# Where the operands of TensorE lie in SBUF, modulo 512 bytes: activations and three block sums change places

## The chip, the cores and the metric

The kernel runs on one core of one Trainium2 chip. Time is device microseconds of one execution, from runs on the chip; three runs of the kernel before gave 1962.86, 1964.51 and 1965.04 us. Lower is better. SBUF is the on-chip memory that the engines read: each of its 128 partitions is a row of bytes, and "address" below is the byte within a partition at which a buffer begins.

## The reference

One decoder layer in float32 on 512 tokens of 2048 features. What is computed:

```python
proj = x @ w_in                               # 2048 -> 4180, split among four head groups
mix  = concat(pooling, conv module, DSA attention, NSA attention)
x = LN(alpha * x + mix @ w_out)               # 2048 x 2048
gate, up = split(x @ w_gate_up)               # 2048 -> 2 x 5632
x = LN(alpha * x + (silu(gate) * up) @ w_down)  # 5632 -> 2048
```

The last two lines, the feed-forward part, are where the change has its largest place.

## The kernel before

**Three products for one.** Each large matrix is used in two parts, a high part (the float32 rounded to the matmul type fp32r) and a low part (the rest). A product is made of three passes that accumulate in PSUM: high by high, high by low, low by high. So every tile of weights is a triple of matmuls, on three lines of code that follow one another. A matmul has a stationary operand (128x128, loaded into the array by its own weight load, LDWEIGHTS, PEld in the profile) and a moving operand (128x256 or 128x512) that streams through.

**Stages in order.** (1) The input projection, `feature_slab` and `part_slab`, lines 799 to 801 through the helper `passes`: stationary is a "whole slab" of weights (`w_hi`, `w_lo`), moving the activations `act`, 512 columns. (2) The attention and pooling parts, on other buffers. (3) The output projection, `out_tile`, lines 1034 to 1036: stationary `act`, moving the slab, 512 columns; in its last quarter two of four slabs lie in `spare_1` and `spare_2`, which are parts of `x_room`. (4) The first two gate and up chunks, again lines 799 to 801: the first pair in halves of 256 columns, the second in 512; the slab of one of them lies in `xs_4`. (5) From 710 us to 1906 us the feed-forward part: 42 chunk units and 20 down units, in the order that `ff_units` writes out (three chunks, two downs, one chunk, and again).

**A chunk unit** makes gate and up of 128 features by seven block products instead of eight (Strassen's scheme). Each is 8 weight tiles by 3 passes = 24 matmuls of 256 columns, on lines 1152, 1154 and 1156 (`product`). The stationary operand is always a piece of the weight ring (`ring_hi`, `ring_lo`, in `w_room`). The moving operand is: product 0, `act`; products 1 and 2, the block sums s1 and s2 in `x_room`; product 3, the block sum s4 in `xs_4` (the trace writes xs); product 4, the block sum s3, which is kept in `act`; products 5 and 6, `act`. So 4 of 7 have `act` as moving operand and 3 of 7 the sums in `x_room` and `xs_4`.

**A down unit** has seven block products of 12 matmuls of 512 columns, lines 1201, 1203 and 1205: stationary the hidden blocks (`h01`, `h23`, `hs4`, `hs21`), moving the weight ring. The tail (lines 1241 to 1243) is the last part of the down product, with moving operands from the ring and from `late`, which begins at the start of `x_room`.

**Who feeds the ring.** SP issues the DMAs, ACT writes the high part (line 1490), VectorE the low part (line 2041) and the weights' block sums (lines 2049 to 2056). Semaphores count all of it, and each engine's order is written out by hand.

**Where the buffers lie.** Buffers are laid out one after the other, so a constant early in the layout moves what follows. `w_room` begins at byte 2240, which is 192 modulo 512. The ring is cut from its start in pieces of 4096 bytes, the low half 512 bytes further, so every piece of the ring is at 192 modulo 512. `SHIFT` (floats, 4 bytes each) says how far past the ring's start the whole slabs begin, and, since `act` and `raw` follow `w_room` and `between` fills up to a fixed sum, also where these two lie. `X_SHIFT` says how far past the start of `x_room` (192 modulo 512) the block sums s1 and s2 begin; `xs_4` and the rows of gain and bias follow `x_room`. The matmul operands step from tile to tile by multiples of 512 bytes, so an operand keeps its place modulo 512.

| buffer | used as | before, mod 512 | past the ring | after, mod 512 | past the ring |
|---|---|---|---|---|---|
| weight ring | stationary (chunk), moving (down, tail) | 192 | 0 | 192 | 0 |
| `w_hi`, `w_lo` whole slabs | stationary (1, 4), moving (3) | 224 | 32 | 256 | 64 |
| `act` (also holds s3) | moving (1, 4, chunk), stationary (3) | 224 | 32 | 256 | 64 |
| s1, s2 and the spare slabs in `x_room` | moving (chunk, 3) | 256 | 64 | 224 | 32 |
| s4 / a slab in `xs_4` | moving (chunk), stationary (4) | 256 | 64 | 224 | 32 |
| hidden blocks, `late` in `x_room`, `raw_c`, `proj` | as named above | 192 | 0 | 192 | 0 |

Of the kernel before, what the change touches and what calls it, by code (L numbers as in the profile page):

```python
# [98 lines left out]


GRAN = SLAB // 2
SHIFT = 8
X_SHIFT = 144
HALF_TOKS = SEQ // 2
S_ORDER = ("s1", "s2", "s4", "s3")
TAIL_SLOTS = ((0, 32), (2, 32), (4, 63), (5, 63), (1, 32), (3, 32), (0, 33), (2, 33))
# [36 lines left out]
def build(nc, x, x_t, w_in, w_out, pool_w, pool_scale, conv_w, conv_b, conv_ln_g, conv_ln_b, conv_pw_w,  # L143
          conv_pw_b, cmp_pos_k, cmp_pos_v, cmp_k_w1, cmp_k_w2, cmp_v_w1, cmp_v_w2, ln1_g, ln1_b,
          ln2_g, ln2_b, w_gate_up, w_down, out):
    with ExitStack() as ctx:
        def sb(name, shape, dt=F32, where=ctx):
            return where.enter_context(nc.sbuf_tensor(name, shape, dt))

        def sem(name):  # L150
# [5 lines left out]
        std = sb("std", [P, TT])  # L156
        w_room = sb("w_room", [P, 4 * SLAB + P + SHIFT], F32R)
        w_hi, w_lo = (w_room[:, SHIFT + at:SHIFT + at + 2 * SLAB].rearrange("p (s n) -> p s n", s=2)
                      for at in (0, 2 * SLAB + P))
# [3 lines left out]

        between = sb("between", [P, P - SHIFT])

# [50 lines left out]
        with a2_scope:  # L216
            below_s1 = sb("below_s1", [P, X_SHIFT], F32, a2_scope)
            s1 = sb("s1", [P, KT // 2, HALF_TOKS], F32, a2_scope)
            below_a2 = sb("below_a2", [P, SLAB], F32, a2_scope)
            a21 = sb("a21", [P, KT // 2, HALF_TOKS], F32, a2_scope)  # L220
            a22 = sb("a22", [P, KT // 2, HALF_TOKS], F32, a2_scope)
        x_room = sb("x_room", [P, 4 * SLAB + X_SHIFT], F32R, feed)
        xs_1, xs_2 = (x_room[:, X_SHIFT + at:X_SHIFT + at + 2 * SLAB].rearrange("p (a k n) -> p a k n", a=2, n=HALF_TOKS)
                      for at in (0, 2 * SLAB))
# [5 lines left out]
        with s4_scope:  # L230
# [22 lines left out]
        spare_1, spare_2 = ((x_room[:, at:at + SLAB], x_room[:, at + SLAB:at + 2 * SLAB])  # L253
                            for at in (X_SHIFT, X_SHIFT + 2 * SLAB))
        spare_4 = tuple(xs_4[:, a, :, :].rearrange("p k n -> p (k n)") for a in range(2))
# [2005 lines left out]
```

How the kernel before makes its waits and increments, by code:

```python
        def copied(eng, n):  # L451
            eng.wait_ge(bank_free[n % 2], n // 2 + 1)
# [1 line left out]
        def tile_ready(eng, group, slab, i):  # L455
            if i < TT - 1:
                eng.wait_ge(tile_done, group * (TT - 1) + (i + 1))
            else:
                eng.wait_ge(slab_done, slab + 1)
# [4 lines left out]
        @block.sync  # L465
# [19 lines left out]
            rows = ((conv_w[0], 0, CONV_WIDTH), (conv_b, V_CB, 1), (conv_ln_g, V_LG, 1),  # L485
                    (conv_ln_b, V_LB, 1), (conv_pw_b, V_PB, 1), (pool_scale, V_PS, 1))
            for src, at, n in rows:
                nc.sync.dma_start(sel[at:at + n, 0:SEQ], src).then_inc(small_loaded, 16)
            nc.sync.dma_start(sel[0:CMP_BLOCK, SEQ:SEQ + P], cmp_pos_k[0]).then_inc(small_loaded, 16)
            nc.sync.dma_start(sel[CMP_BLOCK:2 * CMP_BLOCK, SEQ:SEQ + P], cmp_pos_v[0]).then_inc(small_loaded, 16)
            nc.sync.dma_start(w2[:, 0, :], cmp_k_w2[0]).then_inc(small_loaded, 16)
            nc.sync.dma_start(w2[:, 1, :], cmp_v_w2[0]).then_inc(small_loaded, 16)
            for n in (2, 3):
                sp.wait_ge(part_lo, n + 3)
                load(n % 2, win[:, :, C_IQ + n * P:C_IQ + (n + 1) * P], KT)
            sp.wait_ge(split_done, N_IKWG - 1)
            ikwg = raw[:, 0, 0:KT * (W_IKW + W_NG)].rearrange("p (k n) -> p k n", k=KT)
# [2 lines left out]
            with sp.Fori(0, 4) as c:
                sp.wait_ge(split_done, 2 * c + (N_CONV - 1))
                load(1, win[:, :, bass.ds(c * P + C_G, P)], KT)
```

## Time and profile before

| | us |
|---|---|
| median of three runs (lowest, highest) | 1964.51 (1962.86, 1965.04) |
| the profiled execution's own time | 1964.08 |
| its span | 1962.2 |
| PE busy | 1952.2 (99%) |
| PE weight loads | 1731.7 (88%) |
| VectorE, ACT, POOL busy | 1412.2, 848.4, 504.1 |

The 1.9 us between the time and the span lie around the program's own instructions. TensorE's granted clock is 1.0 in every slice, which is its upper level of 2.4 GHz. The "mean ns" of a matmul group is the length of one matmul with its way through the array, and matmuls overlap; what a matmul costs a stream is the distance from its start to the start of the next. That distance is read in the timeline, as the difference of two start times divided by the number of matmuls between.

### The profile page before, as it was taken

Reading aid. Unit: us, or ns where it says so; the run is one execution under the profiler, and the core shown is the slowest. Engines: PE = TensorE matmul, PEld = TensorE weight load, DVE = VectorE, ACT = ScalarE, POOL = GpSimd, SP = SyncE. Lnnn points to the kernel's source line nnn. Section 1 sums busy time; section 2 is a strip of 40 time slices with the busy share of each in tenths; the row PEclk is TensorE's granted clock in tenths of the full one; section 3 lists DMA queues with packets and bytes.
Section 4 is the critical chain, followed back from the end, with each engine's and each line's share of the span. In section 5 each row is a group of like instructions: output and inputs, shape, how many; then the busy total and the mean of one; then the engine's idle time right before and its main releaser. Section 6 shows DMA issues by size and latency. Waiting matters only on the chain.

```text
span 1962.2 us, 30226 instructions
## 1 busy us (share of the span) xinstructions
PE 1952.2 (99%) x12301; PEld 1731.7 (88%) x12301; DVE 1412.2 (72%) x1911; ACT 848.4 (43%) x1280; POOL 504.1 (26%) x343
## 2 busy tenths in 40 slices
PE   9999999999999999999999999999999999999998
PEld 7777888866888999998989999899998989999896
DVE  3079997274112988887878888888788888878777
ACT  3011001265000545556565555655555555555553
POOL 2555656244567310202011020201102020110200
PEclk9999999999999999999999999999999999999999
DMA  7433343500524524938557394754839376493972
GB/s 214 105 89 80 92 103 90 177 21 25 214 86 131 170 65 129 184 118 166 136 130 172 114 187 126 156 149 116 186 98 203 111 158 152 111 200 90 204 244 87
DMA packets 316429, 264.28 MB, mean 135 GB/s; under 512 B 12262, under 2 KB 258854, under 8 KB 313482
## 3 DMA queue, kind: packets, MB, share of 16 engines
q1 hardware_dynamic: 292026, 211.97, 37.7%
q0 software_dynamic: 23616, 46.15, 14.1%
q10 hardware_dynamic: 656, 4.33, 0.6%
q8 instruction: 93, 1.52, 0.3%
q14 instruction: 38, 0.31, 0.1%
HBM read 211.95 MB, written 50.33 MB: 134 GB/s over the span
## 4 chain that ended last, share of the span: by engine, by line
PE 96%; DMA 1%; DVE 1%; ACT 1%; issue 0%; SPq 0%; DVEq 0%
PE psum L1152 14%; PE psum L1156 14%; PE psum L1154 14%; PE psum L799 7%; PE psum L801 7%; PE psum L800 7%; PE psum L1201 6%; PE psum L1203 6%; PE psum L1205 6%; PE psum L1034 3%; PE psum L1035 3%; PE psum L1036 3%; PE psum L1013 1%; PE psum L950 1%; PE psum L941 1%; PE psum L1001 1%
## 5 line engine op out<-in xcount | busy, mean ns | idle before, releaser
L2041 DVE TENSOR_TENSOR w_room<-raw,w_room 128x1024 fp32r<-128x1024 f32 x310 | 379.5, 1224 | 158.9 <-ACT w_room L1490 158.8
L1490 ACT CAST w_room<-raw 128x1024 fp32r<-128x1024 f32 x312 | 329.1, 1055 | 211.3 <-DVE raw L2052 70.3
L769 POOL DMA_DIRECT2D out<-stage x160 | 139.5, 1472 | 1017.5 <-DVE stage L2152 996.8
L1152 PE MATMUL psum<-act,w_room 128*128 128x256 f32 x1344 | 375.7, 280 | 0.0
L1154 PE MATMUL psum<-act,w_room 128*128 128x256 f32 x1344 | 375.4, 279 | 0.0
L1156 PE MATMUL psum<-act,w_room 128*128 128x256 f32 x1344 | 375.3, 279 | 0.0
L1152 PEld LDWEIGHTS psum<-act,w_room 128*128 128x128 f32 x1344 | 252.6, 188 | 0.4
L1154 PEld LDWEIGHTS psum<-act,w_room 128*128 128x128 f32 x1344 | 252.6, 188 | 0.4
L1156 PEld LDWEIGHTS psum<-act,w_room 128*128 128x128 f32 x1344 | 252.8, 188 | 0.0
L799 PE MATMUL psum<-act,w_room 128*128 128x512 f32 (+2 forms) x608 | 231.8, 381 | 1.7 <-DVE act L1716 1.2
L800 PE MATMUL psum<-act,w_room 128*128 128x512 f32 (+2 forms) x608 | 230.0, 378 | 0.0
L801 PE MATMUL psum<-act,w_room 128*128 128x512 f32 (+2 forms) x608 | 229.9, 378 | 0.0
L677 POOL TENSOR_TENSOR w_room<-raw,w_room 128x2048 fp32r<-128x2048 f32 (+1 forms) x45 | 207.4, 4609 | 3.8
L1152 PE MATMUL psum<-x_room,w_room 128*128 128x256 f32 x672 | 185.6, 276 | 0.0
L1156 PE MATMUL psum<-x_room,w_room 128*128 128x256 f32 x672 | 185.5, 276 | 0.0
L1154 PE MATMUL psum<-x_room,w_room 128*128 128x256 f32 x672 | 185.5, 276 | 0.0
L2041 DVE TENSOR_TENSOR w_room<-raw_c,w_room 128x1024 fp32r<-128x1024 f32 x124 | 151.6, 1223 | 46.9 <-ACT w_room L1490 45.1
L674 POOL TENSOR_SCALAR w_room<-raw 128x2048 fp32r<-128x2048 f32 (+1 forms) x45 | 88.9, 1975 | 259.5 <-PE psum L801 136.9
L799 PEld LDWEIGHTS psum<-act,w_room 128*128 128x128 f32 (+1 forms) x608 | 113.8, 187 | 26.9 <-issue 4.4
L800 PEld LDWEIGHTS psum<-act,w_room 128*128 128x128 f32 (+1 forms) x608 | 113.8, 187 | 22.1 <-issue 0.5
L801 PEld LDWEIGHTS psum<-act,w_room 128*128 128x128 f32 (+1 forms) x608 | 113.8, 187 | 22.1
L1490 ACT CAST w_room<-raw_c 128x1024 fp32r<-128x1024 f32 x126 | 132.9, 1055 | 0.0
(303 smaller groups left out, 4121.5 us busy)
## 6 DMA issues: line engine op xcount, KB each, us to landing
raw_c<-in_w_gate_up SPq DMA_DIRECT2D x84, 512.0 KB, 6.6
raw<-in_w_gate_up SPq DMA_DIRECT2D x84, 512.0 KB, 5.8
out<-stage POOLq DMA_DIRECT2D x160, 256.0 KB, 8.2
raw<-in_w_in SPq DMA_DIRECT2D x30, 1024.0 KB, 5.8
raw<-in_w_down SPq DMA_DIRECT2D x46, 512.0 KB, 4.8
raw_c<-in_w_down SPq DMA_DIRECT2D x42, 512.0 KB, 4.4
raw<-in_w_out SPq DMA_DIRECT2D x16, 1024.0 KB, 5.1
acc<-in_x SPq DMA_DIRECT2D x1, 4096.0 KB, 12.5
```

The costliest lines, as they stand in the source:

```text
L677: nc.gpsimd.tensor_tensor(lo, raw[:, slot, 0:words], hi.bitcast(F32), ALU.subtract)\
L769: nc.gpsimd.dma_start(out_dram[:, tile, n * SEQ:(n + 1) * SEQ], part, accum_op=ALU.add)\
L799: nc.tensor.matmul(out_ap, stat_hi, mov_hi, start=first, stop=False)
L800: nc.tensor.matmul(out_ap, stat_hi, mov_lo, start=False, stop=False)
L801: return nc.tensor.matmul(out_ap, stat_lo, mov_hi, start=False, stop=last)
L1152: nc.tensor.matmul(out_ap, stat_hi[:, cols], mov_hi[:, k, :], start=opens and k == 0, stop=False, skip_group_check=not opens)
L1154: nc.tensor.matmul(out_ap, stat_hi[:, cols], mov_lo[:, k, :], start=False, stop=False, skip_group_check=not opens)
L1156: mm = nc.tensor.matmul(out_ap, stat_lo[:, cols], mov_hi[:, k, :], start=False, stop=k == kh - 1, skip_group_check=not opens)
L1201: nc.tensor.matmul(out_ap[:, i, :], room[:, 0, j, toks], w_h[:, cols], start=opens and j == 0, stop=False, skip_group_check=not opens)
L1203: nc.tensor.matmul(out_ap[:, i, :], room[:, 1, j, toks], w_h[:, cols], start=False, stop=False, skip_group_check=not opens)
L1490: nc.scalar.copy(ring_hi(at), src).then_inc(hi_ready, 1)
L2041: nc.vector.tensor_tensor(lo, src, hi.bitcast(F32), ALU.subtract).then_inc(lo_ready, 1)
```

## The change

Two constants change. `SHIFT` goes from 8 to 16 floats (32 to 64 bytes), `X_SHIFT` from 144 to 8 floats (576 bytes, which is 64 modulo 512, to 32 bytes). `act` and `raw` begin 32 bytes later, the whole slabs too; s1, s2, the spare slabs, `xs_4` and the gain and bias rows begin 544 bytes earlier. The sequence of instructions is the same on each of the five engines, row for row; only the addresses differ.

```diff
 GRAN = SLAB // 2
-SHIFT = 8
-X_SHIFT = 144
+SHIFT = 16
+X_SHIFT = 8
 HALF_TOKS = SEQ // 2
```

Where they are used:

```python
w_room = sb("w_room", [P, 4 * SLAB + P + SHIFT], F32R)
w_hi, w_lo = (w_room[:, SHIFT + at:SHIFT + at + 2 * SLAB]... for at in (0, 2 * SLAB + P))
between = sb("between", [P, P - SHIFT])
below_s1 = sb("below_s1", [P, X_SHIFT], F32, a2_scope)
x_room = sb("x_room", [P, 4 * SLAB + X_SHIFT], F32R, feed)
```

## Rows read from the trace of the kernel before

**Rows 1.** The page, part 1: busy us (share of the span) xinstructions.
```profile
PE 1952.2 (99%) x12301; PEld 1731.7 (88%) x12301; DVE 1412.2 (72%) x1911; ACT 848.4 (43%) x1280; POOL 504.1 (26%) x343
```

**Rows 2.** Windows: length, busy PE PEld DVE ACT POOL (xinstructions), PEclk, DMA share, GB/s.
```profile
710.50:1905.90 1195.40, 1195.40 (x8738) 1129.67 (x8737) 984.52 (x1113) 672.77 (x914) 142.22 (x166) 1.00 0.62 149
```

**Rows 3.** Timeline of PE, third chunk unit: start, length, engine, line, op, names.
```profile
749.91 0.28 PE L1152 MATMUL psum<-act,w_room 128*128 128x256 f32 x1
...
752.71 0.28 PE L1152 MATMUL psum<-x_room,w_room 128*128 128x256 f32 x1
...
760.88 0.28 PE L1152 MATMUL psum<-act,w_room 128*128 128x256 f32 x1
...
769.29 0.40 PE L1201 MATMUL psum<-w_room,h 128*128 128x512 f32 x1
```

**Rows 4.** Timeline of PE, first and second chunk unit.
```profile
710.54 0.28 PE L1152 MATMUL psum<-act,w_room 128*128 128x256 f32 x1
...
713.34 0.28 PE L1152 MATMUL psum<-x_room,w_room 128*128 128x256 f32 x1
...
721.82 0.28 PE L1152 MATMUL psum<-act,w_room 128*128 128x256 f32 x1
...
730.46 0.28 PE L1152 MATMUL psum<-act,w_room 128*128 128x256 f32 x1
...
733.34 0.28 PE L1152 MATMUL psum<-x_room,w_room 128*128 128x256 f32 x1
```

**Rows 5.** Timeline of PE, end of the second down unit.
```profile
788.35 0.39 PE L1201 MATMUL psum<-w_room,h 128*128 128x512 f32 x1
...
807.39 0.28 PE L1152 MATMUL psum<-act,w_room 128*128 128x256 f32 x1
```

**Rows 6.** Timeline of PE, stage 4: halves, the slab in xs_4, the slab in w_room.
```profile
673.73 0.28 PE L800 MATMUL psum<-act,w_room 128*128 128x256 f32 x1
...
688.00 0.40 PE L799 MATMUL psum<-act,xs 128*128 128x512 f32 x1
...
699.19 0.39 PE L799 MATMUL psum<-act,w_room 128*128 128x512 f32 x1
...
710.08 0.62 PE L1142 MATMUL psum<-act 128*128 128x512 f32 x2
```

**Rows 7.** Timeline of PE, output projection: from w_room, then from x_room.
```profile
500.11 0.39 PE L1034 MATMUL psum<-w_room,act 128*128 128x512 f32 x1
...
624.55 0.40 PE L1034 MATMUL psum<-x_room,act 128*128 128x512 f32 x1
...
630.15 0.40 PE L1034 MATMUL psum<-w_room,act 128*128 128x512 f32 x1
```

**Rows 8.** Timeline of PE, tail: moving operand from late, in x_room.
```profile
1944.98 0.39 PE L1241 MATMUL psum<-x_room,h 128*128 128x512 f32 x1
...
1950.19 0.39 PE L1243 MATMUL psum<-x_room,h 128*128 128x512 f32 x1
```

**Rows 9.** Lines of VectorE and ACT by form, 900 to 1900 us: busy, mean ns, idle before.
```profile
L2041 DVE TENSOR_TENSOR w_room<-raw,w_room 128x1024 fp32r<-128x1024 f32 x259 | 317.1, 1224 | 133.1 <-ACT w_room L1490 133.0
L2041 DVE TENSOR_TENSOR w_room<-raw_c,w_room 128x1024 fp32r<-128x1024 f32 x104 | 127.2, 1223 | 41.3 <-ACT w_room L1490 39.9
...
L1490 ACT CAST w_room<-raw 128x1024 fp32r<-128x1024 f32 x260 | 274.2, 1055 | 176.9 <-DVE raw L2052 60.6 <-DVE raw L2049 54.7 <-PE psum L1156 48.8
L1490 ACT CAST w_room<-raw_c 128x1024 fp32r<-128x1024 f32 x104 | 109.7, 1055 | 0.0
```

**Rows 10.** Lines of PE by form, whole span: busy, mean ns, idle before.
```profile
L1152 PE MATMUL psum<-act,w_room 128*128 128x256 f32 x1344 | 375.7, 280 | 0.0
...
L1152 PE MATMUL psum<-x_room,w_room 128*128 128x256 f32 x672 | 185.6, 276 | 0.0
...
L799 PE MATMUL psum<-act,w_room 128*128 128x256 f32 x64 | 18.3, 286 | 0.0
...
L1034 PE MATMUL psum<-x_room,act 128*128 128x512 f32 x32 | 12.7, 398 | 0.0
```

## Prediction

> **What bounds the kernel now.** I read the page's first part, then one sum over the feed-forward part, then the timeline. TensorE is busy for 1952.2 of 1962.2 us [rows 1]; from 710.5 to 1905.9 us it never stops (1195.40 of 1195.40 us, granted clock 1.00, the upper level of 2.4 GHz), while VectorE works 984.5 and ACT 672.8 us of it [rows 2]. So in 61% of the span no wait can be removed, and none is near: the time is the number of matmuls times the distance from one start to the next. The change alters no instruction, only addresses, so it can act through that distance alone.
>
> The distance is read from start times. In the third chunk unit [rows 3] the 24 matmuls of product 0 (moving operand in `act`) take 749.91 to 752.71 = 2.80 us, 116.7 ns each; the 72 of products 1 to 3 (moving in `x_room`, `xs_4`) take 8.17 us, 113.5 ns; the 72 of products 4 to 6 (moving in `act` again) 8.41 us, 116.8 ns. Same shape, same stationary ring, same clock; the moving operand's place differs: 32 bytes past the ring in `act`, 64 in the sums. That is the only term of size.
>
> **Is it the place, or the buffer?** Four other readings say the place. (a) Same two buffers, 256 columns, but a whole slab in place of a ring piece, hence offset 0 between stationary and moving: 673.73 to 688.00, 119 matmuls, 119.9 ns [rows 6]. So 0, 32 and 64 bytes give 119.9, 116.7 and 113.5 ns. (b) At 512 columns offset 0 costs nothing over twice 113.3: `act` with `w_room` 226.7 ns (500.11 to 624.55, 549 matmuls) [rows 7], and 226.9 with the roles exchanged (48 matmuls) [rows 6]. (c) `x_room` as moving operand 32 bytes past `act` takes 233.3 ns (24 matmuls) [rows 7], yet the same `x_room` at offset 0 to the hidden blocks takes 226.5 (23 distances) [rows 8]. (d) `act` moving 32 bytes before `xs_4` takes 233.1 (48) [rows 6]. A buffer that is slow in one pairing is at the floor in another. Down units have both operands 192 modulo 512 and run at 226.7 (84 matmuls, 19.04 us) [rows 5]; nothing in them moves.
>
> Here a rule of the Trainium skill speaks against the change. Its page "TensorE: Matmul & The Clock Gate" (step-by-step, on LDWEIGHTS) says that TensorE has two independent read ports and that loading the next weights takes no read bandwidth from the running matmul. By that rule the places of the two operands could not matter and the change would be worth 0. The trace disagrees in so far as the same matmul takes 113.5, 116.8 or 119.9 ns; whether the reads meet in a bank no row shows.
>
> **Part by part.**
>
> 1. *Chunk units, `act` from 32 to 64 bytes past the ring.* Products 4 to 6 go from 8.41 to what products 1 to 3 take now, 8.17; product 0 from 2.80 to a third of 8.17 = 2.72.
> 2. *Chunk units, the sums from 64 to 32.* Products 1 to 3 go from 8.17 to 8.41. Terms 1 and 2 together: a unit goes from 19.38 (749.91 to 769.29) to 2.72 + 8.41 + 8.17 = 19.30. The exchange of three against three cancels; what stays is one product, 4 against 3, at 0.077 us. All on the path, nothing beside it: 42 x 0.077 = -3.2 us. The bound of that term: no trace shows `act` at 64 or the sums at 32, so `act` gives between 0 and 42 x 96 x 3.3 ns = -13.3 us, the sums cost between 0 and 42 x 72 x 3.3 ns = +10.0 us. I take both in full, for (a) to (d).
> 3. *The first two units.* They aren't like the others [rows 4]: products 1 to 3 of unit one run at 117.8 ns (721.82 - 713.34 over 72) at the same addresses that give 113.5 later, products 4 to 6 and the next unit's product 0 at 120.0, and only at 733.34 does the fast pace begin. Unit one takes 19.92 us, unit two 19.45; against 19.38 that is 0.61 us too much. So a pairing has a slow and a fast rhythm (117.8 or 113.5 at 64 bytes; 120.0 or 116.8 at 32), which the stream falls into by how it arrives, and keeps. After the change the stream arrives otherwise: between 0 and -0.6 us; I take -0.3.
> 4. *Whole slabs with `act`* (input projection, most of the output projection, the first chunks). Both move by 32 bytes, the offset stays 0: 0 us. (b) and the down units show offset 0 at 226.7 both at 224 and at 192 modulo 512, so the absolute place isn't what counts. If 256 in place of 224 did lift the half-width pairs of [rows 6] to 113.5, it would be 119 x 6.4 ns = -0.8 us.
> 5. *Spare slabs in `x_room`, slab in `xs_4`.* The first go from +32 to -32 relative to `act`, the second from -32 to +32. +32 measures 233.3 and -32 233.1, so 96 and 48 matmuls trade nothing: 0 us, 0.1 at most.
> 6. *VectorE, ACT, DMA.* `raw` moves from 224 to 256, `act` too. VectorE's subtraction takes 1224 ns from `raw` (at 224) and 1223 from `raw_c` (at 192), ACT's cast 1055 from both [rows 9]: their place costs nothing. They get 0.08 us less per unit of 19.38 and VectorE is busy 82% of the stretch [rows 2], so no wait opens; were VectorE the limit, it would show as TensorE's first idle time there.
>
> Sum: -3.2 - 0.3 = -3.5 us. The profiled execution took 1964.08 us (span 1962.2 and 1.9 around it); it would take 1960.6. The median of the three runs lies 0.4 higher at 1964.51: forecast 1961.0 us, a span of 1958.7. What a measurement of this kernel tells from no change is about 0.2%, here 3.9 us, so the forecast sits just short of that edge.
>
> **Rivals.**
>
> *R1, the slow rhythm after each down group (no change).* Product 0 after a down unit is reached from a stream at 226.7 ns. At 32 bytes it settles at once at 116.8; at 64 nobody has seen this entry. If it falls into 117.8 as in unit one, product 0 costs 24 x 4.4 ns = 0.11 more, products 1 to 3 follow at 120.0 as products 4 to 6 did there, 72 x 3.2 = 0.23, and product 4 escapes as at 733.34. Eleven entries (the start and ten down groups) x 0.34 = +3.7, against -3.2: 1965.0. For it: unit one. Against: the rows hold one entry into 64 bytes that ends slow (713.34) and two that end fast, 733.34 from the slow rhythm [rows 4] and 752.71 from the fast one [rows 3].
>
> *R2, the penalty belongs to `act`, and the sums catch one too (slower).* `act` steps by 2048 bytes between weight tiles, the sums by 1024, and `act` lies next to the ring. If that is what makes 116.8, `act` stays there at 64 bytes, while the sums at 32 rise to it: 42 x 72 x 3.3 ns = +10.0, 1974.5 us. It decides if product 0 stays at 116 ns or more. Against it: (a), where the same buffers give 119.9 at another offset.
>
> *R3, the slow rhythm everywhere (slower).* Units of 96 x 117.8 + 72 x 120.0 ns = 19.95 against 19.38: 42 x 0.57 = +24, 1988 us. Against it: each entry from `act` to the sums after unit one is fast, and after the change product 4 is entered in just that way, 32 to 64 bytes, after a multiple of 24 matmuls.
>
> *R4, the sums don't mind 32 bytes.* Their tiles lie closer; then only term 1 counts: -13.3, 1951 us. For it: only `act` has been seen at 32 with the ring. Against: (c), (d).
>
> *R5, the places don't matter* (the rule of the page named above would give this time too): 1964.5 us. Against it: (a) to (d).
>
> **How the numbers follow.** The exchange as worked out 58%, R1 18%, R4 8%, R2 8%, R3 3%, R5 5%. The first gives -3.2 to -4.6 us, with terms 3 and 4 at their ends, and the three runs spread over 2.2 us, so the edge at -3.9 cuts it near the middle: 27 of the 58 fall over 0.2% faster, 31 within. Faster: 27 + 8 = 35%. Same: 31 + 18 + 5 = 54%. Slower: 8 + 3 = 11%. The range 1957.5 to 1966.5 holds the first, R1 and R5, 81%; R2, R3 and R4 lie outside.
>
> **What would show it.** In the timeline of the third unit after: product 0 in 2.72 us, products 1 to 3 in 8.41, products 4 to 6 in 8.17, the unit in 19.30. In the groups by line, the mean for `act` at L1152 falls from 280 to 276 ns and that for x_room rises from 276 to 280, while the spare slabs at L1034 stay at 398 and the halves at L799 at 286 [rows 10]. Units one and two tell of term 3, product 0 after 807 us of R1. The forecast is wrong if product 0 keeps 116 ns or more (R2), if products 1 to 3 stay at 113.5 (R4), or if TensorE waits anywhere in the stretch.

## The result, and the profile after

The changed kernel takes 1975.61 us (median of five runs, 1974.66 to 1976.75) against 1964.51 (1962.86 to 1965.73): ratio 1.0058, 95% interval 1.0044 to 1.0073. It is slower by 11 us (0.6%), where -3.5 was forecast and 1957.5 to 1966.5 given as the range. The profiled execution took 1975.12 us with a span of 1973.3.

The page's first row, then a window over nearly the whole feed-forward part (its first matmul starts at 709.98, the first of the tail at 1917.96), answer to [rows 1, 2]:

```profile
PE 1963.8 (100%) x12301; PEld 1744.1 (88%) x12301; DVE 1411.3 (72%) x1911; ACT 845.5 (43%) x1280; POOL 503.6 (26%) x343
...
709.90:1917.60 1207.70, 1207.70 (x8735) 1141.78 (x8734) 984.47 (x1114) 671.17 (x915) 141.93 (x166) 1.00 0.59 148
```

TensorE still never stops there, its clock is still at the upper level, VectorE and ACT do the same work. The loss is in the distance between matmuls: the stretch from the first chunk unit to the tail took 1905.85 - 710.54 = 1195.31 us before and takes 1917.96 - 709.98 = 1207.98 now, +12.7. What lies ahead of it is 0.56 us shorter, what lies behind 1.0 us; together +11.1, the difference of the spans. The 0.56 us can't be told from chance: in the traces of the kernels below unit one begins between 708.85 and 711.94 us, and at 711.50 in the one with extra matmuls, whose program is the changed kernel's up to there. Behind the stretch the kernel before takes 11.93 us for the first 48 matmuls of its tail (1905.85 to 1917.78), the changed one 10.92. 0.6 of this 1.0 us is one wait for VectorE before the matmul at 1908.50, which the slower kernel doesn't have.

The timeline of TensorE, unit one to three and the first after the downs (start, length, engine, line, op, names), answers to [rows 3, 4]:

```profile
709.98 0.28 PE L1152 MATMUL psum<-act,w_room 128*128 128x256 f32 x1
...
712.81 0.28 PE L1152 MATMUL psum<-x_room,w_room 128*128 128x256 f32 x1
...
721.45 0.28 PE L1152 MATMUL psum<-act,w_room 128*128 128x256 f32 x1
...
748.90 0.28 PE L1152 MATMUL psum<-act,w_room 128*128 128x256 f32 x1
...
751.62 0.28 PE L1152 MATMUL psum<-x_room,w_room 128*128 128x256 f32 x1
...
759.92 0.28 PE L1156 MATMUL psum<-xs,w_room 128*128 128x256 f32 x1
760.03 0.28 PE L1152 MATMUL psum<-act,w_room 128*128 128x256 f32 x1
...
768.20 0.39 PE L1201 MATMUL psum<-w_room,h 128*128 128x512 f32 x1
...
806.32 0.28 PE L1152 MATMUL psum<-act,w_room 128*128 128x256 f32 x1
...
809.15 0.28 PE L1152 MATMUL psum<-x_room,w_room 128*128 128x256 f32 x1
...
817.43 0.28 PE L1156 MATMUL psum<-xs,w_room 128*128 128x256 f32 x1
817.55 0.28 PE L1152 MATMUL psum<-act,w_room 128*128 128x256 f32 x1
...
826.03 0.28 PE L1152 MATMUL psum<-act,w_room 128*128 128x256 f32 x1
...
923.27 0.28 PE L1152 MATMUL psum<-act,w_room 128*128 128x256 f32 x1
```

Unit three is the forecast to the hundredth: product 0 in 2.72 us, products 1 to 3 in 8.41, products 4 to 6 in 8.17, the unit in 19.30. Then come the first two down units (38.12 us, before 38.10), and the unit behind them keeps another pace: 2.83, 8.40 and 8.48 us, or 117.9, 116.7 and 117.8 ns, 19.71 us. From here to the end each act product runs at 117.8 ns, at the same addresses that gave 113.3 ns sixty microseconds earlier. A group (four chunk units and two down units) takes 923.27 - 806.32 = 116.95 us; before it took 115.59 (807.39 [rows 5] to 922.98). That is 0.34 us a unit; 39 units are +13, and the first three give 0.5 back.

The groups by line hardly show it (columns: busy us, mean ns of one, idle before):

```profile
L1152 PE MATMUL psum<-act,w_room 128*128 128x256 f32 x1344 | 376.1, 280 | 0.0
L1152 PE MATMUL psum<-x_room,w_room 128*128 128x256 f32 x672 | 187.6, 279 | 0.0
...
L1034 PE MATMUL psum<-x_room,act 128*128 128x512 f32 x32 | 12.7, 398 | 0.0
```

Against [rows 10] the sums rose from 276 to 279, where 280 was forecast, and act stayed at 280, where 276 was. A mean over the program hides that act ran at 113.3 ns in most of the first three units and at 117.8 in the other 39.

### The profile page after: what moved, and what is told of

It reads as the page before. It is cut to its first block, busy times and chain, and to the rows that moved or that the text cites. A ratio compares the mean times of both kernels' runs of the same rounds, so it can differ in the third digit from the quotient of the medians.

```text
span 1973.3 us, 30226 instructions
## 1 busy us (share of the span) xinstructions
PE 1963.8 (100%) x12301; PEld 1744.1 (88%) x12301; DVE 1411.3 (72%) x1911; ACT 845.5 (43%) x1280; POOL 503.6 (26%) x343
## 4 chain that ended last, share of the span: by engine, by line
PE 98%; DVE 1%; DMA 0%; ACT 0%; issue 0%; SPq 0%; DVEq 0%
PE psum L1152 14%; PE psum L1156 14%; PE psum L1154 14%; PE psum L799 7%; PE psum L801 7%; PE psum L800 7%; PE psum L1201 6%; PE psum L1205 6%; PE psum L1203 6%; PE psum L1034 3%; PE psum L1036 3%; PE psum L1035 3%; PE psum L1013 1%; PE psum L950 1%; PE psum L941 1%; PE psum L1001 1%
## 5 line engine op out<-in xcount | busy, mean ns | idle before, releaser
L1154 PE MATMUL psum<-x_room,w_room 128*128 128x256 f32 x672 | 187.7, 279 | 0.0
L1156 PE MATMUL psum<-x_room,w_room 128*128 128x256 f32 x672 | 187.6, 279 | 0.0
L1152 PE MATMUL psum<-x_room,w_room 128*128 128x256 f32 x672 | 187.6, 279 | 0.0
```

Source lines behind the costliest of these rows:

```text
L1152: nc.tensor.matmul(out_ap, stat_hi[:, cols], mov_hi[:, k, :], start=opens and k == 0, stop=False, skip_group_check=not opens)
L1154: nc.tensor.matmul(out_ap, stat_hi[:, cols], mov_lo[:, k, :], start=False, stop=False, skip_group_check=not opens)
L1156: mm = nc.tensor.matmul(out_ap, stat_lo[:, cols], mov_hi[:, k, :], start=False, stop=k == kh - 1, skip_group_check=not opens)
```

## Experiments

Theory T says: the distance depends on the place of the moving operand to the stationary one and on a rhythm that the stream holds. At 64 bytes there is a fast rhythm (113.3 ns) and a slow one (117.8), at 32 bytes 116.7 and 120.0. Which one holds is settled where the stream arrives from another place or width, and stays until it leaves. Rival A: the slow pace belongs to the act buffer. Rival B: it belongs to what begins with the down units beside TensorE, such as the accumulating DMAs. "Phase" below is the step of a repeating pattern at which the stream stands when it crosses to another place.

### TensorE alone, every place

A kernel of its own that leaves the whole layer out and only copies x to the output. Its streams, shortened:

```python
for step in range(16):            # every place modulo 512
    wide(12)                      # 12 matmuls of 512 columns, both operands at one place
    narrow(72, ma, 32 * step)     # 72 of 256 columns, moving operand 32*step bytes past the ring
for mid in (72, 71, 73, 74):
    wide(12); narrow(24, ma, 64); narrow(mid, mb, 32); narrow(72, ma, 64)
for mid in (24, 25, 26, 27):
    wide(12); narrow(mid, mb, 32); narrow(48, ma, 64)
for mid in (24, 6, 3):
    wide(12); narrow(mid, mb, 0); narrow(48, ma, 64)
```

> This kernel computes nothing of the layer: it copies x to the output and beside it lets TensorE run streams of matmuls alone, with VectorE, ACT, POOL and DMA idle, on buffers laid out as in the kernel (ring at 192 modulo 512, high and low tiles in triples). For each of the 16 places of the moving operand, 0 to 480 bytes past the ring, 12 matmuls of 512 columns are followed by 72 of 256; then come crossings 64 to 32 to 64 with 72, 71, 73 and 74 matmuls in the middle, 32 to 64 after 24 to 27, and 0 to 64 after 24, 6 and 3. Theory T (place and rhythm): 0 bytes 120 ns from start to start, 32 bytes 116.7, 64 bytes 117.8 when entered from 512 columns, as in the changed kernel after down units; the crossing with 72 gives 117.8 at the end, and one of 71, 73 and 74 gives 113.3, since the phase in which the stretch at 32 ends decides. Rival A (the activations' buffer is slow by its own place): in buffers that are not act, 64 bytes gives 113.3 by every entry. Rival B (what begins with the down units beside TensorE, the accumulating DMAs above all, slows it): with all else idle 64 bytes gives 113.3 throughout.

The timeline of TensorE in this kernel; the view merges equal matmuls, so a row is a stream with its count, and its pace is the next row's start less its own, over the count. First the places 0, 32 and 64, then place 256, then the crossings with 72 and 71 in the middle, then 24 and 25 at 32 bytes:

```profile
36.05 8.80 PE L72 MATMUL psum<-ma,ring 128*128 128x256 f32 x72
44.68 2.91 PE L59 MATMUL psum<-ring,hid 128*128 128x512 f32 x12
47.43 8.56 PE L72 MATMUL psum<-ma,ring 128*128 128x256 f32 x72
55.83 2.91 PE L59 MATMUL psum<-ring,hid 128*128 128x512 f32 x12
58.58 8.64 PE L72 MATMUL psum<-ma,ring 128*128 128x256 f32 x72
67.06 2.92 PE L59 MATMUL psum<-ring,hid 128*128 128x512 f32 x12
...
126.39 8.80 PE L72 MATMUL psum<-ma,ring 128*128 128x256 f32 x72
135.02 2.91 PE L59 MATMUL psum<-ring,hid 128*128 128x512 f32 x12
...
219.56 8.56 PE L72 MATMUL psum<-mb,ring 128*128 128x256 f32 x72
227.96 8.64 PE L72 MATMUL psum<-ma,ring 128*128 128x256 f32 x72
236.44 2.92 PE L59 MATMUL psum<-ring,hid 128*128 128x512 f32 x12
...
242.03 8.45 PE L72 MATMUL psum<-mb,ring 128*128 128x256 f32 x71
250.31 8.33 PE L72 MATMUL psum<-ma,ring 128*128 128x256 f32 x72
258.47 2.91 PE L59 MATMUL psum<-ring,hid 128*128 128x512 f32 x12
...
306.48 2.96 PE L72 MATMUL psum<-mb,ring 128*128 128x256 f32 x24
309.29 5.60 PE L72 MATMUL psum<-ma,ring 128*128 128x256 f32 x48
314.72 2.91 PE L59 MATMUL psum<-ring,hid 128*128 128x512 f32 x12
317.47 3.08 PE L72 MATMUL psum<-mb,ring 128*128 128x256 f32 x25
320.39 5.82 PE L72 MATMUL psum<-ma,ring 128*128 128x256 f32 x48
326.05 2.92 PE L59 MATMUL psum<-ring,hid 128*128 128x512 f32 x12
```

By place, entered from 512 columns, in ns from start to start, each from such a pair of rows:

| bytes past | 0 | 32 | 64 | 96 | 128 | 160 | 192 | 224 |
|---|---|---|---|---|---|---|---|---|
| ns | 119.9 | 116.7 | 117.8 | 120.0 | 120.0 | 118.7 | 117.8 | 118.3 |

The places 256 to 480 repeat these eight (256 bytes: 135.02 - 126.39 over 72 = 119.9). 64 bytes, reached in this way, is slow, with VectorE, ACT, POOL and DMA idle and in a buffer that isn't act: both rivals fall. With 72 matmuls at 32 bytes before it, 64 bytes runs at 117.8 (227.96 to 236.44), with 71 at 113.3 (250.31 to 258.47); 73 and 74 gave 117.8. From 24 matmuls at 32 bytes, entered from 512 columns, the crossing is fast (309.29 to 314.72 over 48 = 113.1), from 25 slow (117.9); 26 and 27 were fast and slow again. From 0 bytes all three were slow. So a single matmul more or less ahead of a crossing can settle the pace of the whole stream that follows.

### Another number of matmuls at each group of the changed kernel

```diff
+EXTRA = {3: (0, 0), 7: (0, 1), 11: (0, 2), 15: (0, 3), 19: (1, 0), ...}
                 stat_hi, stat_lo = ring_hi(un.q + e), ring_lo(un.q + e)
+                for _ in range(EXTRA.get(un.m, (0, 0))[e] if e < 2 else 0):
+                    nc.tensor.matmul(out_ap, stat_hi[:, 0:P], mov_hi[:, 0, :], start=True, stop=True)
```

> The changed kernel, with the first matmul of product 0 or 1 issued again up to four times in the chunk unit that follows each down group (it opens its sum anew each time, so the result is the same); each of the ten groups gets another number: product 0 / product 1: 0/0, 0/1, 0/2, 0/3, 1/0, 2/0, 3/0, 4/0, 1/3, 0/4. That shifts the phase in which the stream crosses to the next place. Theory T: in at least one of the shifted groups (the one with three more at product 1 above all, since the four-step pattern at 32 bytes then ends one step earlier) products 4 to 6 and every following act product until the next down group run at 113.3 ns, the unit at 19.30 us; in group one (0/0) they stay at 117.8, the unit at 19.70. Rivals A and B: all ten groups stay at 117.8, whatever is repeated.

The timeline at the group with three more at product 1: its start, product 4, the next unit's product 1, the next group's start:

```profile
1157.69 0.28 PE L1155 MATMUL psum<-act,w_room 128*128 128x256 f32 x1
...
1169.27 0.28 PE L1155 MATMUL psum<-act,w_room 128*128 128x256 f32 x1
...
1180.15 0.28 PE L1155 MATMUL psum<-x_room,w_room 128*128 128x256 f32 x1
...
1273.44 0.28 PE L1152 MATMUL psum<-act,w_room 128*128 128x256 f32 x1
```

From 1169.27 to 1180.15 the 96 act matmuls take 10.88 us, 113.3 ns, and the fast rhythm holds to the group's end. The group takes 1273.44 - 1157.69 = 115.75 us with the three added, against 116.95 where nothing was added (807.87 to 924.82). The others (added at product 0/product 1): 1/0, 4/0 and 1/3 had the fast rhythm from product 4 of their first unit as well, 0/1 and 2/0 in the second unit, 0/2 in the third, and 0/0, 3/0 and 0/4 never. It came each time out of the slow rhythm at 32 bytes (120.0 ns), except for 0/3. (0/4 stands in the last group, which has three units.) A single run took 1971.68 us.

How a pace keeps itself can be read in the starts, which the trace holds to the nanosecond. At 32 bytes the distances follow one of three patterns, in ns: 116, 117, 117 behind the down units and behind the 512 columns in the kernel with TensorE alone; behind a stream at 64 bytes, 120, 113, 116, 118 over and over, or 120 throughout. The counts that follow are over every crossing in the traces of both kernels, of TensorE alone, of this kernel and of the two below that repeat or lead with a matmul at each group (before_plus1, after_lead2). Of the crossings from 32 to 64 bytes out of the four-step pattern, 95 of 95 that left on the short step (113) were fast, and 88 of 88 that left on another step were slow; out of 120 throughout, 11 of 11 were fast. The rows of the changed kernel's timeline in the section on the result show one of each: unit three leaves for act on a step of 0.11 us (759.92 to 760.03), the unit after the downs on one of 0.12 (817.43 to 817.55).

Behind a fast stream at 64 bytes the short step is the 8th, the 12th and so on, so also the 72nd and the 96th (105 of 105 stretches); behind a slow one it is the 3rd, the 7th and so on to the 71st and the 75th (96 of 109; in 11 the pattern is 120 throughout, in 2 the short step stands elsewhere). Apart from product 0 behind 512 columns, the stretches at 32 bytes are 72 matmuls after the change and 96 before it, multiples of four: as a rule fast leaves fast behind it, and slow leaves slow. Of the lengths 71 to 76 behind a slow stream, only 71 and 75 (0/3) crossed fast. What in the chip makes the pattern stays open.

### All at 64, all at 32

```diff
-SHIFT = 8
-X_SHIFT = 144
+SHIFT = 16        # both64
+X_SHIFT = 144
...
+SHIFT = 8         # both32
+X_SHIFT = 8
```

> SHIFT 16 and X_SHIFT 144: activations and sums both 64 bytes past the ring. Theory T: all seven products share one place, so the rhythm that the first takes is kept: 117.8 ns in every product after the downs, a unit 168 x 117.8 = 19.79 us against 19.38 before, about 1981 us. Place alone, without rhythm (what the prediction assumed): 168 x 113.4 = 19.05 us a unit, 1951 us. Rival A: act at 117.8, sums at 113.4: 96 x 117.8 + 72 x 113.4 = 19.47, 1968 us.

> SHIFT 8 and X_SHIFT 8: activations and sums both 32 bytes past the ring. Theory T: a stream entered from a down unit keeps 116.7 ns in all seven products, a unit 168 x 116.7 = 19.61 us against 19.38: +9.5, about 1974 us. Rival A (only act pays): 19.38, 1964.5 us. If the slow rhythm at 32 (120.0) took over after the downs: 20.16 a unit, 1997 us.

Timeline of TensorE, both at 64 bytes, the first unit after the first downs:

```profile
806.32 0.28 PE L1152 MATMUL psum<-act,w_room 128*128 128x256 f32 x1
...
826.11 0.28 PE L1152 MATMUL psum<-act,w_room 128*128 128x256 f32 x1
```

19.79 us over 168 matmuls, 117.8 ns; 1978.75 us (1977.83 to 1980.74), ratio 1.0080 [1.0063, 1.0097]. With no change of place inside a unit the slow rhythm is never left. Both at 32, the same unit:

```profile
808.88 0.28 PE L1152 MATMUL psum<-act,w_room 128*128 128x256 f32 x1
...
828.48 0.28 PE L1152 MATMUL psum<-act,w_room 128*128 128x256 f32 x1
```

19.60 us, 116.7 ns; 1973.37 us (1971.90 to 1973.42), ratio 1.0048 [1.0031, 1.0064]. That the sums, too, run at 116.7 when they lie 32 bytes past the ring is what the forecast had assumed.

### Leading matmuls at 32 bytes

All operands at 64 bytes, and before product 0 some matmuls whose moving operand begins 32 bytes earlier:

```diff
+LEAD = {0: 2, 3: 1, 7: 2, 11: 3, 15: 4, 19: 5, 23: 6, 27: 8, 31: 10, 35: 12, 39: 24}
+            at = 9 * SEQ - 8
+            lead_in = act_hi.rearrange("p k s -> p (k s)")[:, at:at + HALF_TOKS]
+                for _ in range(LEAD.get(un.m, 0) if e == 0 else 0):
+                    nc.tensor.matmul(out_ap, stat_hi[:, 0:P], lead_in, start=True, stop=True)
```

> SHIFT 16 and X_SHIFT 144 (all moving operands of the chunk units 64 bytes past the ring, where all ran at 117.8 ns), and before product 0 of the first unit and of each unit that follows a down group some matmuls of 256 columns whose moving operand begins 8 floats earlier, so 32 bytes past the ring; their sum is opened anew by product 0, so the result is the same. Numbers: first unit 2, then by group 1, 2, 3, 4, 5, 6, 8, 10, 12, 24. Theory T: a few of them put the stream into the fast rhythm at 64 bytes, which then holds for all four units of the group: 113.3 ns, a unit 168 x 113.3 = 19.04 us against 19.38 before; in the sweep 24 and 26 did and 25 and 27 did not, so I expect the even numbers and 24 for certain. Rival (the slow pace at 64 belongs to what runs beside the down units, or to act): all groups stay at 117.8, 19.79 a unit, whatever leads.

Timeline, the starts of the groups with one, two and three leads:

```profile
808.18 0.28 PE L1154 MATMUL psum<-act,w_room 128*128 128x256 f32 x1
...
925.56 0.28 PE L1154 MATMUL psum<-act,w_room 128*128 128x256 f32 x1
...
1040.07 0.28 PE L1154 MATMUL psum<-act,w_room 128*128 128x256 f32 x1
```

One lead: 117.38 us a group (slow throughout). Two: 114.51, with all four units at 113.3 ns. Three and five were slow; four, six, eight, ten, twelve and twenty-four fast. The two leads of the first unit did nothing, which I hadn't expected. That unit is reached from two matmuls on act alone and not from a down unit, and in the kernel before its product 0 at 32 bytes ran in the four-step pattern, where odd and even don't decide, while behind the down units it ran in the other. A single run took 1969.02 us.

### The kernel before, with one matmul issued twice

```diff
+EXTRA = {m: (1, 0) for m in range(3, 43, 4)}
```

(with the same loop as above, on the kernel before)

> The kernel before, with one change: the first matmul of product 0 is issued twice in the ten chunk units that follow a down group, so 25 matmuls at 32 bytes stand before the crossing to 64 instead of 24 (the sum is opened anew, the result is the same). Work added: 10 x 0.117 = 1.2 us. Theory T: as in the sweep (25 gave 117.9 after the crossing), products 1 to 3 of these units run at 117.8 ns, products 4 to 6 and the next product 0 at 116.7 or 120.0, and the fast pace comes back at a later crossing: 0.3 to 0.75 us a group, 4 to 8.7 us in all with the added matmuls, 1967.5 to 1972. Rival (place alone decides, by whatever mechanism): 1.2 us, 1964.7.

Timeline: the first unit after the downs, its products 1 and 4, the next unit's product 1, the next group:

```profile
807.49 0.28 PE L1152 MATMUL psum<-act,w_room 128*128 128x256 f32 x1
...
810.41 0.28 PE L1155 MATMUL psum<-x_room,w_room 128*128 128x256 f32 x1
...
818.89 0.28 PE L1155 MATMUL psum<-act,w_room 128*128 128x256 f32 x1
...
830.09 0.28 PE L1155 MATMUL psum<-x_room,w_room 128*128 128x256 f32 x1
...
924.45 0.28 PE L1152 MATMUL psum<-act,w_room 128*128 128x256 f32 x1
```

Products 1 to 3 take 8.48 us, 117.8 ns, where they had 113.3 to 113.5, and keep that in all four units of the group: 116.96 us a group against 115.59. The time is 1977.18 us (1976.06 to 1978.55) against 1964.70, ratio 1.0069 [1.0053, 1.0086]. Ten matmuls of 0.117 us cost 12.5 us. The direction was expected, the size was 1.4 to 3 times too small: I let the fast rhythm come back at a later crossing, and in these ten groups it didn't. The starts say why: the later stretches at 32 bytes are 96 matmuls in the four-step pattern, and each was left on a step other than the short one.

### The changed kernel and both-at-64, with leads

```diff
+LEAD = {m: 2 for m in range(3, 43, 4)}                                  # after_lead2: SHIFT 16, X_SHIFT 8
+LEAD = {m: 3 if m == 0 else 2 for m in (0, *range(3, 43, 4))}           # lead3_2: SHIFT 16, X_SHIFT 144
+LEAD = {m: 1 if m == 0 else 2 for m in (0, *range(3, 43, 4))}           # lead1_2
```

> The changed kernel (act at 64, sums at 32) with two leading matmuls of 256 columns at 32 bytes before product 0 of the ten chunk units that follow a down group. Theory T: the stream enters 64 bytes in the fast rhythm and crosses to 32 and back as the first three units of the changed kernel did after 721 us: act products at 113.3 ns, sums at 116.7, a unit 19.30 us in place of 19.70. A group then takes 4 x 19.30 + 38.1 + 0.3 = 115.6 us against 116.95 in the changed kernel: 1975.6 - 13 = 1962 to 1964 us, so the whole loss of the change is gone. Rivals A and B (act's own place, or what runs beside): 1975.6 plus 10 x 2 x 0.117 = 1978 us.

> All moving operands of the chunk units 64 bytes past the ring, with three leading matmuls at 32 bytes before the first unit and two before each of the ten units after a down group. From the groups with two leads already seen (925.56 to 1040.07 = 114.51 us, against 115.6 in the kernel before): 10 x -1.1 = -11; the first three units at 19.8 if three leads fail as two did (+0.6), at 19.1 if they work (-1.3). Theory T: 1952 to 1954 us, 0.5 to 0.65% faster than before. Rival (something gives it back elsewhere, as the ring then being late): 1964.

> As the kernel with three leads before the first unit, but with one there. Tells only which number before the first unit gives the fast rhythm: the first three units at 113.3 or 117.8 ns; with 117.8 the time is 2 us above a kernel where they run at 113.3.

Two leads in the changed kernel: a group from 805.93 to 921.47,

```profile
805.93 0.28 PE L1154 MATMUL psum<-act,w_room 128*128 128x256 f32 x1
...
921.47 0.28 PE L1154 MATMUL psum<-act,w_room 128*128 128x256 f32 x1
```

115.54 us in place of 116.95; 1961.81 us (1960.71 to 1963.01, ten runs) against 1964.46, ratio 0.9984 [0.9975, 0.9994]. Twenty added matmuls remove 13.8 us from 1975.61. In the stretch itself, from unit one to the tail, the profiled execution takes 1903.84 - 709.60 = 1194.24 us against 1195.31 in the kernel before: -1.1 us with 2.3 us of added work in it, or -3.4 without, where terms 1 to 3 said -3.5. The rest of the -2.7 lies outside the stretch, most of it ahead of unit one, where the start varies as said above.

All at 64 bytes with two leads, a group:

```profile
806.89 0.28 PE L1154 MATMUL psum<-act,w_room 128*128 128x256 f32 x1
...
921.41 0.28 PE L1154 MATMUL psum<-act,w_room 128*128 128x256 f32 x1
```

114.52 us, and 1952.55 us in all (1952.08 to 1955.25): ratio 0.9941 [0.9927, 0.9955], faster than both kernels by 0.6% and 1.2% (the second from the medians, 1952.55 to 1975.61). Of the 11.4 us between the profiled spans (1950.8 and 1962.2), 9.6 lie in the stretch (1894.78 - 709.05 = 1185.73 us against 1195.31) and 1.5 ahead of unit one, which the placement may not have earned. The first three units stayed at 117.8 ns with three leads, and with one as well (1951.70 us in a single run), so some 2 us are left there: 3 x (19.79 - 19.04). TensorE stands still nowhere in the stretch.

## Why the prediction was wrong

- *The bound.* Right. TensorE is the only path through the feed-forward part, before, after and in each experiment on the whole layer, and the change acted by the distance alone.
- *Place, not buffer; terms 1 and 2.* Right in mechanism and size for the fast rhythm: unit three at 19.30 us in its three parts as worked out, and both32 shows the sums at 116.7. The rule of the Trainium skill that was weighed ("TensorE: Matmul & The Clock Gate", "Step-by-step: what each phase is for", that loading the next weights takes no SBUF read bandwidth from the running matmul) was read as saying that the places can't matter. They do: with the other engines idle, the place of the moving operand to the stationary one moves the distance from 116.7 to 120.0 ns. Whether the weight load takes that time from the matmul, no run shows.
- *The step that failed:* in term 1, that act at 64 bytes takes in all 42 units the pace that the sums had there. It holds in the units that the stream enters in the right phase, and the entry from a down unit isn't one: 117.8 ns. Term 1 alone was set at 96 matmuls x -3.3 ns a unit; in 39 units it was about +1.0 ns, from 116.8 to 117.8. That makes 96 x 1.0 ns = +0.1 us where -0.3 was set; term 2 cost its forecast 0.24, and the two together are the +0.34 us a unit.
- *R1 had the place and the entry right and the price wrong.* It named this slow entry after each down group, with 18%, and let it end at product 4, because that had been seen at 733.34. But that escape led out of the slow rhythm at 32 bytes (120.0). Here the sums run at 116.7 and not at R1's 120.0, and the crossing back at product 4 finds the wrong step each time, as at 713.34 before. A loss of 0.34 us in each of 39 units, instead of one unit in four, turned no change into +11. The rows held both crossings from 32 to 64 bytes, the fast at 752.71 and the slow at 713.34; I counted them as odds, and didn't look at the single starts, where the trace of the kernel before already had the four-step pattern: left on its short step at 752.71, on another at 713.34.
- *R2* gave nearly this time (1974.5), by luck: its cause is another. Unit three, the stream without act, and after_lead2 show that act at 64 bytes runs at 113.3 ns. Its mark, product 0 at 116 ns or more, can't tell it from R1; the text said it could.
- *R3, R4, R5* didn't occur; of R3 the slow pace of act did (117.8), that of the sums (120.0) only in unit one. Term 3 came out as taken: the first three units take 58.22 us (709.98 to 768.20) against 58.75 (710.54 to 769.29), and of the -0.53 terms 1 and 2 have 3 x -0.08, which leaves -0.3, though unit one still starts slow. Terms 4 to 6: spare slabs 398 ns as before, VectorE and ACT unchanged, no wait.

## What to carry to other kernels

Where TensorE never waits, read the distance from start to start per stream in the timeline, not the mean length of a group: between the fast and the slow rhythm at 64 bytes the distance differs by 4% (113.3 and 117.8 ns), the mean length by 1.4% (276 and 280). Two settings of one layout are comparable only if the streams are entered alike, so look at each entry (from another width, from another place, after a stall) for a second, lasting pace. If there is one, a matmul or two whose result is thrown away can buy the better pace for the next hundreds, as here; try even and odd counts, and look at the single starts for a pattern and its length.

## What the runs showed of the hardware

- With fp32r operands, 128-column weights and 256-column moving operands, the distance depends on the moving operand's place to the stationary one modulo 256 bytes: 116.7 to 120.0 ns as entered from 512 columns, 113.3 as the best found (at 64 bytes only; whether the other places have a faster rhythm wasn't tried). That it is the place to the stationary operand, and not the place in SBUF, rests on distance 0 alone: 119.9 to 120.0 ns with both operands at 192 modulo 512 (TensorE alone, 36.05 to 44.68), at 224 [rows 6] and, after the change, at 256 (673.14 to 687.42, 119 matmuls).
- The pace has more than one stable value at one place, and holds it for 672 matmuls and more (both64; the four units of a fast group). From 32 to 64 bytes, the step of the four-step pattern (120, 113, 116, 118 ns) on which the stream leaves decided the pace in 183 of 183 crossings. What carries the pattern is open; no run looked inside it.
- At 512 columns a place of 0 ran at 226.7 ns once under way, in the pairings of the output projection, the down units and the tail, and 32 bytes to either side at 233. In the kernel with TensorE alone, twelve such matmuls behind a stream of 256 columns took 0.00 to 0.05 us more than 12 x 226.7 ns.
- One matmul more in ten places cost 12.5 us, and two more in ten places brought 13.8.
